# Expert products in plain f32 on four column strips of TensorE, 96 tokens a tile, in place of three f32r products of split parts

## The reference, cut to what matters

```
logits = xt @ router_w + router_b
top_vals, top_idx = top_k(logits, 4);  gates = softmax(top_vals)
gu   = ragged_dot(xs, w_gu, group_sizes) + b_gu[sorted_e]     # 1024 -> 2048 per expert
gate = minimum(gu[:, ::2], 7);  up = clip(gu[:, 1::2], -7, 7)
act  = (up + 1) * gate * sigmoid(1.702 * gate)
y    = ragged_dot(act, w_down, group_sizes) + b_down[sorted_e] # 1024 -> 1024 per expert
out  = zeros.at[tok].add(y * gates)
...
gate = sigmoid(rms_norm(h) @ ple_gate_w);  h = h + gate * (p @ ple_proj_w)
```

## Time and profile before

| | us |
|---|---|
| median of three runs | 2598.49 |
| lowest and highest run | 2596.66, 2603.37 |
| profiled execution, from its first instruction to its last | 2598.0 |
| of it busy: TensorE matmul | 2528.4 |
| TensorE weight load (beside matmuls) | 2090.3 |
| VectorE | 1962.3 |
| ScalarE | 1352.5 |
| GpSimd | 253.9 |

### The profile page before, as it was taken

One profiled execution on the slowest core, in us unless ns is written; L12 is line 12 of the kernel. 1 busy time (PEld: TensorE's weight loads), 2 busy tenths in 40 slices (PEclk: granted clock), 3 DMA queues, 4 the chain that ended last, 5 costly groups with the idle time before them and its releaser, 6 DMA issues.

```text
span 2598.0 us, 34894 instructions
## 1 busy us (share of the span) xinstructions
PE 2528.4 (97%) x12322; PEld 2090.3 (80%) x12322; DVE 1962.3 (76%) x1942; ACT 1352.5 (52%) x1364; POOL 253.9 (10%) x385
## 2 busy tenths in 40 slices
PE   9998899999999999999998889999999999999998
PEld 7777788888888888888887678888888888888886
DVE  7878999999999999999997887788633445433432
ACT  5233777777777777777776454322221223222222
POOL 2150110000000000000000402021000000000000
PEclk9999999999999999999999999999999999999999
DMA  8545999999999999999997857387433631233332
GB/s 323 205 106 189 327 407 411 400 393 392 394 391 396 394 392 393 393 390 398 393 390 260 208 175 239 91 267 242 131 106 89 162 97 33 65 97 97 109 90 77
DMA packets 346912, 656.52 MB, mean 253 GB/s; under 512 B 28192, under 2 KB 213408, under 8 KB 345824
## 3 DMA queue, kind: packets, MB, share of 16 engines
q1 hardware_dynamic: 319680, 545.03, 60.0%
q0 software_dynamic: 20944, 86.52, 9.3%
q10 hardware_dynamic: 6224, 24.12, 2.3%
HBM read 625.26 MB, written 34.55 MB: 254 GB/s over the span
## 4 chain that ended last, share of the span: by engine, by line
PE 73%; issue 15%; DVE 6%; DMA 3%; ACT 1%; POOL 0%; SPq 0%; ACTq 0%; POOLq 0%; DVEq 0%
PE bank L2622 40%; PE bank L2910 8%; PE bank L2918 7%; PE bank L2911 7%; PE bank L2610 1%; PE bank L2598 1%; PE bank L2605 1%; DMA ring<-in_w_in 1%; DVE slot_lo L1911 1%; PE bank L2416 1%; PE bank L2445 1%; PE bank L2447 1%; PE bank L2446 1%; DVE cb L1564 1%; DMA rows<-in_w_ffn_in 1%
## 5 line engine op out<-in xcount | busy, mean ns | idle before, releaser
L1911 DVE TENSOR_TENSOR slot_lo<-ring,slot_hi 128x2048 fp32r<-128x2048 f32 x384 | 863.7, 2285 | 33.0 <-ACT slot_hi L1112 32.7
L1112 ACT ACTIVATE slot_hi<-ring 128x2048 fp32r<-128x2048 f32 x384 | 736.3, 1921 | 253.1 <-PE bank L2622 225.6
L2622 PE MATMUL bank<-slot_hi,xs_hi 128*128 128x512 f32 x1024 | 316.8, 391 | 0.0
L2622 PE MATMUL bank<-slot_hi,xs_lo 128*128 128x512 f32 x1024 | 315.8, 390 | 0.0
L2910 PE MATMUL bank<-h_hi,fin_hi 128*128 128x512 f32 x704 | 274.4, 390 | 2.0 <-DVE fin_lo L2204 1.9
L2622 PE MATMUL bank<-slot_lo,xs_hi 128*128 128x512 f32 x1024 | 274.1, 389 | 0.0
L2911 PE MATMUL bank<-h_hi,fin_lo 128*128 128x512 f32 x704 | 273.9, 389 | 0.0
L2622 PEld LDWEIGHTS bank<-slot_hi,xs_lo 128*128 128x128 f32 x1024 | 192.5, 188 | 40.9
L2622 PEld LDWEIGHTS bank<-slot_hi,xs_hi 128*128 128x128 f32 x1024 | 192.5, 188 | 40.2
L2622 PEld LDWEIGHTS bank<-slot_lo,xs_hi 128*128 128x128 f32 x1024 | 192.2, 188 | 40.3
L1379 ACT ACTIVATE fin_hi<-rows 128x1024 fp32r<-128x1024 f32 x88 | 88.2, 1052 | 214.8 <-DMA rows<-in_w_ffn_in 214.8
(11 more groups left out here) (486 smaller groups left out, 4079.6 us busy)
## 6 DMA issues: line engine op xcount, KB each, us to landing
ring<-in_expert_w_gate_up SPq DMA_DIRECT2D x256, 1024.0 KB, 8.1
ring<-in_expert_w_down SPq DMA_DIRECT2D x128, 1024.0 KB, 7.1
rows<-in_w_ffn_in SPq DMA_DIRECT2D x88, 512.0 KB, 5.0
work<-in_w_ada POOLq DMA_DIRECT2D x64, 384.0 KB, 4.2
y_dram<-cb ACTq DMA_DIRECT2D x32, 512.0 KB, 7.6
ring<-in_w_ada POOLq DMA_DIRECT2D x36, 384.0 KB, 6.1
work<-in_w_ffn_out SPq DMA_DIRECT2D x8, 1408.0 KB, 7.0
rows<-in_w_ffn_out SPq DMA_DIRECT2D x8, 1408.0 KB, 7.0
```

What stands on the lines that cost most here:

```text
L1112: act.activation(hi_of(e, j), slot[q], ACT.Copy).then_inc(s_slot_hi, 1)
L1911: tt(slot_lo[:, q], slot[q], whole(hi_of(e, j)), ALU.subtract).then_inc(s_slot_lo, 1)
L2622: last = mm(ps[banks + n], x[:, k, :], (lo if lower else hi)[:, k, 512 * n:512 * (n + 1)], start=(begins and lower == 0 and k == 0 and x i ...
```

## The change

- **Products.** `CAP = 96` rows a tile, in three groups of 32. For each slice of 128 input rows and each group, four plain-f32 matmuls hold the same 32 tokens on four strips of 32 columns of the array, and each streams another quarter of the weight columns: 512 for gate/up, 256 for down. Outputs lie on partitions 32c to 32c + 31 of the PSUM banks 0 to 2 (gate/up) and 3 to 5 (down), one bank for a group. No part is split: `split_high`, `split_low`, `tokens_low`, `hidden_low`, `matmuls`, `biases` and the one-hot selector go.
- **Slots.** A gate/up slot is one slice of 128 rows by 2048 columns, a down slot two neighbouring rows on a partition: one run of 8 KB each.
- **Bias and SwiGLU.** VectorE turns and spreads the bias row over partitions (`stream_shuffle`), adds it to all 1536 columns out of PSUM in one instruction, and works on the copy in SBUF, 768 columns an instruction.
- **Results** are 3 x 256 columns on 128 partitions and go out in four stores for each tile, in runs of 1 KB.
- **Order.** TensorE turns hidden columns and the next tokens behind gate/up slot 3. The last expert is written out behind the loop; its hidden columns come before the last slot of the down product ahead of it, and its own result goes to banks 0 to 2.
- **Behind the loop.** ScalarE's last `store_y` comes behind both `ple_weights`. SyncE issues the second half of the PLE weights ahead of `ple_p_sb`. VectorE does `gate_weights_low(1)` ahead of `add_down_bias`, whose pairs of banks are taken in the order 2, 3, 0, 1.
- **Routing** counts tiles of 96 (up to 21 extra ones in place of 15).

The core of the diff follows, in the order SyncE, ScalarE, VectorE, TensorE, VectorE.

```diff
-        slot = [ring[:, 2048 * s:2048 * (s + 1)].rearrange("p (k n) -> p k n", k=2) for s in range(12)]
+        slot = [ring[:, 2048 * s:2048 * (s + 1)] for s in range(12)]
+        down_slot = [slot[8 + d].rearrange("p (two n) -> p two n", two=2) for d in range(4)]
...
-        dn_v = a["expert_w_down"][0].rearrange("e (k p) n -> p e k n", p=P)
+        dn_v = a["expert_w_down"][0].rearrange("e (c p two) n -> p e c (two n)", c=4, two=2)
...
+                src = gu_v[:, e, q, :] if q < 8 else dn_v[:, e, q - 8, :]
+                load(slot[q], src.rearrange("p e n -> p (e n)"), s_slot_in[q])
...
             load(ple_w_sb[0], ple_gate_v[:, :, 0:512], s_ple_in)
+            sp.wait_ge(s_ple_in, 32)
+            load(ple_w_sb[1], ple_gate_v[:, :, 512:1024], s_ple_in)
             sp.wait_ge(s_xst_ready, extra * 2 + 2 * E + 2)
             load(ple_p_sb, ple_proj_v, s_side_in)
-            sp.wait_ge(s_ple_in, 32)
-            load(ple_w_sb[1], ple_gate_v[:, :, 512:1024], s_ple_in)
...
+            def store_y(tile, done, src):
                 act.wait_ge(s_slot_done, done)
+                act.wait_ge(s_y_stored, tile * 64 + 16)
+                act.activation(y_sb, src, ACT.Copy).then_inc(s_y_sb, 1)
+                act.wait_ge(s_y_sb, tile + 2)
+                for c in range(4):
+                    at = y_dram[bass.ds(tile * CAP, CAP), CHUNK // 2 * c:CHUNK // 2 * (c + 1)]
+                    act.dma_start(at.rearrange("(g t) n -> t g n", g=GROUPS), y_sb[32 * c:32 * (c + 1), :, :]).then_inc(s_y_stored, 16)
+            def expert(e, stores=True):
+                if stores:
+                    store_y(e - 2, done_at(e - 1, 11) + 1, hid_ps)
+                tokens_columns(e + 1, done_at(e, 7) + 1)
+                sigmoid(e)
...
             ple_weights(0)
             act.wait_ge(s_ple_in, 48)
             ple_weights(1)
+            store_y(extra + (E - 1), extra * 12 + 12 * E, last_ps)
...
+            def add_bias(tile, done):
+                dve.wait_ge(s_slot_done, done)
+                tt(gate_up, up_ps, bias_bc.unsqueeze(1).broadcast_to([P, GROUPS, CHUNK]), ALU.add).then_inc(s_gate_up, 1)
+            def expert(e):
+                hidden_copy(e - 1, hid_ps)
+                step.until(turn_bias())
+                state_part(e)
+                step.until(spread_bias())
+                add_bias(e, done_at(e, 7) + 1)
+                swiglu(e)
...
+            def up(k, landed):
+                pe.wait_ge(s_slot_in[k], landed)
+                for g in range(GROUPS):
+                    for c in range(4):
+                        last = mm(ps[g][32 * c:32 * (c + 1), :], xs_t[:, k, 32 * g:32 * (g + 1)], slot[k][:, CHUNK * c:CHUNK * (c + 1)],
+                                  start=(k == 0), stop=(k == KD - 1))
                 last.then_inc(s_slot_done, 1)
+            def down(d, landed, first, hidden=hid_t):
+                pe.wait_ge(s_slot_in[8 + d], landed)
+                n = CHUNK // 2
+                for k in range(2):
+                    for g in range(GROUPS):
+                        for c in range(4):
+                            last = mm(ps[first + g][32 * c:32 * (c + 1), 0:n], hidden[:, g, P * k + 32 * d:P * k + 32 * (d + 1)],
+                                      down_slot[d][:, k, n * c:n * (c + 1)], start=(d == 0 and k == 0), stop=(d == 3 and k == 1))
+                last.then_inc(s_slot_done, 1)
+            def expert(e, ends=False):
                 pe.wait_ge(s_xst_ready, e * 2 + 2)
+                pe.wait_ge(s_gate_up, e)
+                for k in range(4):
+                    up(k, e * 16 + 16)
+                pe.wait_ge(s_y_sb, e)
+                hidden_columns(e - 1, 3)
                 tokens_columns(e + 1)
+                for k in range(4, 8):
+                    up(k, e * 16 + 16)
+                pe.wait_ge(s_hid, e)
+                for d in range(4):
+                    if ends and d == 3:
+                        hidden_columns(e, 0)
+                    down(d, e * 16, 3)
...
             gate_weights_low(0)
+            gate_weights_low(1)
             for i in range(NT):
                 add_down_bias(i)
-            gate_weights_low(1)
```

More of the change, by code:

```diff
@@ L436, in program @@
         s_prep_dve = sem("prep_dve")
-        s_pick = sem("pick")
         s_h_hi = sem("h_hi")
@@ L1114, in high_ahead @@
-            def high_ahead(e, j):
-                if is_split(e, j) and is_split(*ahead_of(e, j)):
-                    split_high(*ahead_of(e, j))
-            def pick_biases(index):
-                for n in range(2):
-                    of = slice(2 * E * n, 2 * E * (n + 1))
-                    act.activation(pick[of, n, :], pick_e[of, bass.ds(index, 1)].broadcast_to([2 * E, P]), ACT.Copy).then_inc(s_pick, 1)
-            def sigmoid(tile, h, done):
-                act.wait_ge(s_slot_done, done)
-                if not (isinstance(tile, int) and tile == 0):
-                    act.wait_ge(s_act_ready, tile * 2 + (h - 1))
-                act.activation(t_s[h], pairs[h][:].rearrange("p (f two) -> p f two", two=2)[:, :, 0],
-                               ACT.Sigmoid, scale=ALPHA).then_inc(s_sig_ready, 1)
@@ L1193, in _ @@
                 act.activation(gates_of, ps[4][0:E, :], ACT.Copy).then_inc(s_prep_act, 1)
[L1194 removed]
+            tokens_columns(1, 8)
+            sigmoid(0)
+            expert(1, False)
             act.wait_ge(s_k_out, 16 * (CH + 1))
[L1196 to L1201 removed]
+            with act.Fori(2, E) as e:
+                expert(e)
+            store_y(E - 2, done_at(E - 1, 11) + 1, hid_ps)
             act.wait_ge(s_route_ok, 2)
@@ L1813, in tiles_before @@
                 step(ts(dst, v, float(limit), None, ALU.is_ge))
-                for m in (1, 2):
-                    step(stt(dst, v, float(P * m + limit), dst, ALU.is_ge, ALU.add))
-            tiles_before(need, count, P + 1)
+                for m in range(1, (S - 1) // CAP):
+                    step(stt(dst, v, float(CAP * m + limit), dst, ALU.is_ge, ALU.add))
+            tiles_before(need, count, CAP + 1)
             step(dve.tensor_tensor_scan(total, ones[:, 0:E], need, 0.0, ALU.mult, ALU.add))
@@ L2676, in _ @@
             last.then_inc(s_gates_ps, 1)
-            with pe.Fori(1, E) as e:
+            tokens_columns(1)
+            for k in range(4, 8):
+                up(k, 16)
+            pe.wait_ge(s_prep_act, 2)
+            with pe.Fori(1, E - 1) as e:
                 expert(e)
+            expert(E - 1, ends=True)
             pe.wait_ge(s_xst_ready, 2 * E + 2)
-            hidden_columns(E - 1)
-            hidden_taken(E - 1)
-            pe.wait_ge(s_y_sb, 2 * E - 1)
-            for j in range(4):
-                down(j, hi_of(E, j), split_at(E, j) + 1)
+            pe.wait_ge(s_hid, E)
+            for d in range(4):
+                down(d, E * 16, 0, hid_last)
             pe.wait_ge(s_route_ok, 2)
```

442 lines of the change are left out of this document (128 added, 314 removed).

## The result

The changed kernel takes 2532.84 us (median of 4 runs, 2530.09 to 2534.14); beside it on the same chip the kernel before takes 2597.57 us. The ratio is 0.974, with a 95% interval of 0.973 to 0.976. The profiled execution has a span of 2531.3 us, 66.7 less than before.

What follows compares the result with a forecast made beforehand. TensorE was taken to stay the bound, its period falling from 35.36 to 33.0 us: 73 us won in the loop, 1.4 at its start, 8 lost behind it, so 2598.0 becomes 2531 us; range 2506 to 2564.

Steps and rivals of the forecast that it cites:

- the step that named the bound: Expert loop: weight transfers at 425 GB/s take 32.5 us a period, under TensorE's 33.0, so TensorE stays the bound.
- Matmuls: Expert loop: four strips at once take 215 ns for 512 columns and 108 ns for 256, 31.0 us an expert.
- Rival B: Expert loop: strips overlap only in part; at three strips' worth a period is 43 us, 2840 us in all; chance 0.10.
- 42 us a period: Expert loop: period by the skill's strip speedups, about 0.78 of ideal; above the present period, kept as a rival.
- Transposes and switches: Expert loop: 14 transposes add 1.6 us a period, switches between strips and whole-array transposes 0.4 us.
- Rival A: Expert loop: the weights become the bound; 2544 us at 34.2 us a period, 2565 at 34.9; chance 0.22.
- the lead: Expert loop: loads 8 or 9 slots ahead when issuing resumes, about 23 us of cover against slower DMA.
- The loop's start: Start of the expert loop: expert 1 begins at 306.8 in place of 308.20, 1.4 us won.
- The tail: Behind the loop: first combine 44 us after T0, the end of the last down product but one; 8 us lost.
- The same after: Tail: landing of results to first combine takes 10.7 us by GpSimd's gathers, and the same after the change.
- Rival C: Expert loop: the longer body is fetched anew each pass, up to 235 us, 2648 us at half; chance 0.06.

Runs made afterwards that it cites:

- e3: Changed kernel with the strip as outer and the token group as inner index of the expert loop's matmuls: 2980.38 us, one run.
- e4: Changed kernel with each weight slot loaded by two DMAs of 4 KB rows in place of one with 8 KB rows: 2554.5 us.
- e8: Changed kernel with GpSimd gathering each of the first tiles ahead of the state-table store it stood behind: median 5 us worse.
- e1: Changed kernel with the last expert's result copied out and stored ahead of both PLE weight split halves: median 4.4 us shorter.
- e6: Kernel before, with only the last expert's result store moved behind both PLE weight split halves: 2607.03 us against 2596.82, ratio 1.004.
- e9: Changed kernel with earlier last-result store, second PLE load unwaited, down-bias sums between PLE halves, gathers first, earlier state-kernel stores: 2514.61 us, ratio 0.967.
- e10: Changed kernel with the eight state-kernel stores issued earlier, four by SyncE and four by ScalarE: 1049.4 us from first gate/up matmul to last down product but one.
- e11: e9 with gate/up weights read in 16 KB rows, two slots a load, and token transposes of every eighth column: 2517.65 us.

## Why the prediction was right, and where it was not

The forecast of 2531 us met 2532.84. Its mechanism was right (four strips at once carry the loop, the tail loses some 8 us), but the step that named the bound failed. That the sum came out within 2 us is luck: TensorE's own pace was 31 x 0.43 = 13 us better than forecast, the waits for slots cost 14 and that for a gather some 2 more, and the loop's start gave back 4.

- **Matmuls.** Forecast 215 and 108 ns; measured 10.30/48 = 214.6 and 10.36/96 = 107.9. The overlap is 0.856/0.2146 = 3.99 of 4, even better than the 3.92 of the short stretch in the earlier trace rows. Rival B is out, and e3 shows what it hangs on: the strip as the fastest index.
- The Trainium skill, "TensorE: Matmul & The Clock Gate", section "Measured speedup vs the span model", gives 2.38x for three column strips and 3.07x for four row strips; the prediction's estimate of 42 us a period came from these. 32.57 was measured, so for a steady stream of four 32-column strips the trace disagrees with that ratio.
- **Transposes and switches.** Forecast 1.6 and 0.4 us; measured 0.81 + 0.66 = 1.47, and 10.44 - 10.30 = 0.14 for the half of gate/up that follows the transposes. The period is 32.57 us, not 33.0.
- **The weights: the step that failed.** "I take 425 GB/s ... and 0.4 us for the result store": 32.5 us, "under 33.0, so TensorE stays the bound". The loop runs at 408 to 410, 33.2 to 33.4 us a period, above TensorE's 32.57. The rate of the rows was nearly right, though no row had shown it: 421 GB/s between the dips. The 0.4 us does not show. What was put at nothing is the dip while a gather lands: by the stretches under e4, 13.63 MB at 420 GB/s are 32.5 us, and 4 us at 326 lose 4 x (420 - 326)/420 = 0.9 more, 33.4 in all.
- **What it cost.** Rival A's mechanism came in the second half: once 14 periods at some 0.75 us, about 10 us, had used up the lead (I had put it at 23), 16 periods of 33.44 cost 16 x 0.86 = 14 us. 31 periods came out at a mean of 33.12 against 33.0 forecast, because TensorE's own pace was 0.4 better.
- **The loop's start.** Forecast 1.4 us won, bounds 4 and -2; 5.45 measured, outside them. 3.1 of it is the first matmul, at 278.50 in place of 281.58, the rest expert 0, 24.25 us in place of 26.6. The first part is luck: that matmul's start differs by more from trace to trace (276.7 to 286.2). Not foreseen: the wait for tile 2's gather, and e8 shows that it cost nothing in the end.
- **The tail.** Forecast T0 + 44, loss 8; measured 43.2 and 7.3. From the copy's end to the landing it is 1361.56 - 1358.12 = 3.44 us (some 3, bounds 2 to 5), and from there to the combine 11.1 (10.7). e1 and e6 show the mechanism from both sides. "The same after" did not hold: from the first to the last combine it is 25.5 us, 22.9 before.
- **Rival C.** The instruction queue has 48 packets and no expert begins with idle time (381.02 + 0.66 = 381.68 in the chain), so nothing is fetched in each pass. The Trainium skill, "Runtime: NRT & Kernel Launch", section "Instruction fetch mechanics", speaks of a window of two pages, from which the prediction took 512 instructions; the same section gives TensorE's instruction memory 2048, and a body of about 800 fits in that. The trace agrees with the larger figure.
- VectorE is at 53.20/210 = 25% in the loop, as forecast.

Open: why the early stores in e9 won so little, whether the gather makes the dip in each period, and how many records may wait on a strip.

## What to carry to other kernels

Price the transfers of a loop from a stretch of the trace that has the same mixture of loads, gathers and stores and is long enough to hold a whole period, not from single fast loads: a bound that lies 2% below the next one is not settled. Where a store or a split is moved past a wait, look for what the next engine needs of it; the 7 us of this tail came from one line on ScalarE, and moved back ahead, its store was slowed by the loads beside it. And where DMA sets the end of a loop, a stall removed at its start comes back later.

## What the runs showed of the hardware

- Four strips of 32 columns in turn run plain f32 at 3.99 of 4 for 512 columns; three in a row to the same strip cost 1.46 times as much (e3), not the 2.6 of strict order, for records of other strips start ahead of a waiting one.
- Loads in rows of 4, 8 and 16 KB, in this mixture: 403, 410 and 413 GB/s (e4, the changed kernel, e11, where a third of the bytes stayed in 8 KB rows).
- Small stores beside loads, on another queue and on the same one: beside 8 KB loads on SyncE's queue, four stores of 64 KB in 64-byte pieces, issued by ScalarE, had a median landing of 28.9 us (e10), while 412 to 423 GB/s were moved from 305 to 320 us (347 and 330 in two later stretches of 5 us); on SyncE's own queue (the changed kernel) they landed in a median of 4.3 us, but SyncE issued the eight for 17 us and no load meanwhile.
- TensorE takes up the PLE gate at 1.2 GHz, half of full speed: the granted clock was 0.93 from 1372 to 1378 us, where TensorE was busy for 2.57 of 6, and 0.50 in the stretch below. The gate's first matmuls start 0.43 us apart, later ones 0.23. In the kernel before the clock was 1.00 at that place (1446 to 1450).

```profile
1378.00:1382.00 4.00, 3.31 (x11) 2.70 (x12) 2.08 (x3) 2.34 (x4) 0.15 (x1) 0.50 0.98 397
```

- From 240 to 280 us, ahead of the loop, the mean granted clock was 1.00 in the kernel before, 0.87 in e6, 0.91 in seven of the traces (the changed kernel's two among them) and 0.74 to 0.76 in e3 and e8 to e11; in these five the first gate/up matmul comes 5 to 8 us later. It looks like a matter of the execution and not of the kernel: before and e6 have the same program up to there, and the profiled executions of e8 to e11 took 2 to 11 us more than their kernels' medians. Why the lower level lasts longer there, no run shows.
